# Feed-forward: seven quarter products for the first matrix from the second pair of column groups on, in place of the third

## The chip, the cores and the metric

The kernel runs on one core of a Trainium2 chip. The metric is the device time of one execution in microseconds (us). A run is timed several times and the median is quoted. "TensorE" is the matmul engine (PE in the rows, PEld its weight loads), "VectorE" is DVE, "ScalarE" is ACT, "GpSimd" is POOL, and "SyncE" is SP, whose queue here issues the weight loads from device memory.

## The reference

Two blocks of two layers each are computed one after the other over 512 tokens of width 1024. Only one piece matters here, the feed-forward that closes each of the two layers of the second block:

```python
def swiglu(x, w1, w3, w2):
    return (jax.nn.silu(x @ w1) * (x @ w3)) @ w2

h = h + swiglu(rmsnorm(h, ffn_norm[layer]), ffn_w1[layer], ffn_w3[layer], ffn_w2[layer])
```

`w1` and `w3` are 1024 x 2816, `w2` is 2816 x 1024, everything is float32.

## The kernel before

Activations are kept transposed, features on the 128 partitions and tokens in the free dimension. Every dense product of float32 values is made of three float16 products: each operand is split into a high part (float16) and a low part (the rest, float16), and high x high, high x low, low x high are added in PSUM (`PASSES`). ScalarE writes the high part with a copy, VectorE the low part with a subtraction.

The weights come in groups of 256 columns (two blocks of 128, "column block 0 and 1") of 1024 rows, 1 MB, through a ring of two slots (`m.ring`), filled by SyncE; their high and low parts lie in `m.wsplit`, also two slots. The feed-forward (`ffn_window`) takes the groups in the order w1, w3, w1, w3, ... : a **pair** is one group of w1 (the silu matrix) and one of w3 (the gate matrix), so a pair yields 256 of the 2816 hidden features. There are eleven pairs (`KF // 2`, counted from 0 here).

- The **dense** pairs. For each column block, 8 steps of k times 3 passes of a 128x128 weight with all tokens. Pair 0 does this for the tokens in two halves, EARLY (0 to 255) and LATE (256 to 511), because the norm of the halves ends at different times; pair 1 has all 512 tokens at once. The result of w1 leaves PSUM through a silu on ScalarE (L2880), the result of w3 through a multiplication with it on VectorE (L2883). ScalarE and VectorE then split the hidden values (L2947, L2953).
- The **quick** pairs, class `Seven`. The product of a w1 group (1024 x 256, seen as 2 x 2 quarters B) with the normed input (2 x 2 quarters A: features by token halves) is made with seven quarter products P1 to P7 instead of eight, in the manner of Strassen. Each is 4 steps of k times 3 passes over 256 columns (L2637). They need sums of quarters of both sides: S1, S3, S2, S4 of the input, made once (`combine` L2761 on VectorE, high part L2774 on ScalarE, low part L2781 on VectorE), and T3, T1, T2, T4 of each w1 group (`sum_of` L2699 on VectorE), which are split with the two unsummed parts B11 and B2 in the order `SPLITS` (L2717 on ScalarE, L2724 on VectorE). VectorE adds the products up (L2800, L2805, L2811, L2816), ScalarE copies P1 (L2789) and applies the silus (L2823, L2826). The w3 group of a quick pair is dense over 512 tokens (L2649; split L2736 and L2746, gate L2835, hidden values L2842 and L2850).

The order on TensorE is P1, P2, P6, P7, P5, P3, P4, then gate block 0 and 1. What each needs:

```python
FACTORS = {"P1": ("B11", "A11", "B11"), "P2": ("B21", "A12", "B2"), "P3": ("B22", "S4", "B2"), "P4": ("T4", "A22", "T4"),
           "P5": ("T1", "S1", "T1"), "P6": ("T2", "S2", "T2"), "P7": ("T3", "S3", "T3")}
SPLITS = ("B11", "B2", "T3", "T1", "T2", "T4")
MIXED = ("S1", "S3", "S2", "S4")
```

PSUM has eight banks. The dense parts go round banks 0 to 5: first twelve parts of the residual product before the feed-forward (L2534 stores them), then pair 0's eight (EARLY silu 0, 1, EARLY gate 0, 1, LATE silu 0, 1, LATE gate 0, 1), then in the kernel before pair 1's four. `Seven` puts P1 and P5 in bank 0, P2 and P6 in bank 1, P7 in bank 2, P3 and P4 in bank 3, the gates in banks 4 and 5. In its first pair P1, P2, P7, P3 and the gates wait until the last dense part that used their bank is stored (`before`, which is `earlier` in `ffn_window`). The stores count on two semaphores, one for ScalarE (`da`) and one for VectorE (`dd`).

The order on each engine is written by hand as a table of times: every step `yield`s the time at which it is due, and `weave` merges the steps of an engine's streams by these times when the program is built. The times are a plan only: on the chip each engine runs its instructions in the woven order, with waits on semaphores. The times the change touches are those of `sum_time`, `split_time`, `combine`, `combine_hi` and `combine_lo`. `LED` in `ffn_window` is the number of dense pairs.

## Time and profile before

| | |
|---|---|
| median of 3 runs | 3083.76 us (3080.12 to 3085.23) |
| the profiled execution: its time | 3088.69 us |
| its span in the profile | 3086.9 us |
| TensorE busy | 2950.7 us, 96% |
| VectorE busy | 1836.0 us, 59% |
| ScalarE busy | 1310.4 us, 42% |
| mean granted TensorE clock | 0.984 of 2.4 GHz |

The profile is of one execution; starts are counted from the beginning of its span. The time of a run is a little longer than its span (1.8 us here). The quarter products of the first feed-forward run from 2087 to 2263 us, those of the second from 2784 to 2960 us. The duration of a matmul in a row includes its passage through the array, which overlaps the next one; the pace is read from the distance of starts.

### The profile page before, as it was taken

To read this page: it belongs to the slowest core of one execution; us is meant where nothing else is said; L and a number is where in the kernel's file an instruction comes from. 1 tells how busy PE (TensorE), PEld (TensorE's weight loads), DVE (VectorE), ACT (ScalarE), POOL (GpSimd) and SP (SyncE) were. 2 spreads that over 40 slices of the span, in tenths; PEclk is the share of its full clock that TensorE was granted. 3 is DMA by queue.
4 is the path that set the end of the run, shared out by engine and by line. 5 is a ranking of instruction groups with operands and counts; after the bars stand their busy time and mean duration, and the time that the engine had idled before them with its cause. 6 is when DMAs were issued, how large, how long until landed. Compare 5 with 4: busy or idle time off the path is not lost. (4 is left out here: it accounts for less than half of the span.)

```text
span 3086.9 us, 48857 instructions
## 1 busy us (share of the span) xinstructions
PE 2950.7 (96%) x19588; PEld 1860.2 (60%) x19588; DVE 1836.0 (59%) x3400; ACT 1310.4 (42%) x2743; POOL 35.7 (1%) x108
## 2 busy tenths in 40 slices
PE   7999999999999999999999988999999989999998
PEld 4576867766656466757554454366655666666654
DVE  6337665555534637765665567677734468777744
ACT  3235545443332325455444353444423238744422
POOL 0000000000000000000000000000000001100000
PEclk9999999999999999999999999999999989999999
DMA  8411112211122221122322323223324420023322
GB/s 335 178 59 43 42 62 73 94 68 52 49 105 85 101 86 57 42 90 69 130 82 106 110 95 113 92 83 110 110 94 128 139 74 2 17 94 110 110 94 84
DMA packets 59364, 282.98 MB, mean 92 GB/s; under 512 B 7773, under 2 KB 13533, under 8 KB 38533
## 3 DMA queue, kind: packets, MB, share of 16 engines
q1 hardware_dynamic: 54485, 274.49, 25.6%
q10 hardware_dynamic: 4656, 5.38, 0.5%
q8 instruction: 157, 2.57, 0.3%
q14 instruction: 66, 0.54, 0.1%
HBM read 261.83 MB, written 6.34 MB: 87 GB/s over the span
## 5 line engine op out<-in xcount | busy, mean ns | idle before, releaser
L315 PE MATMUL banks<-h_sb,wsplit_sb 128*128 128x512 f16 (+2 forms) x6528 | 1216.7, 340 | 44.7 <-PEq L86 18.3
L315 PEld LDWEIGHTS banks<-h_sb,wsplit_sb 128*128 128x128 f16 x6528 | 634.0, 99 | 537.5 <-issue 68.5
L315 PE MATMUL banks<-quads,wsplit_sb 128*128 128x512 f16 (+2 forms) x3300 | 587.4, 337 | 4.6 <-PEq L86 4.6
L300 DVE SCALAR_TENSOR_TENSOR wsplit_sb<-ring_sb,wsplit_sb 128x1024 f16<-128x1024 f32 (+2 forms) x356 | 382.5, 1090 | 251.6 <-ACT wsplit_sb L290 249.5
L290 ACT ACTIVATE wsplit_sb<-ring_sb 128x1024 f16<-128x1024 f32 (+2 forms) x356 | 330.1, 944 | 469.0 <-PE banks L315 419.4
L315 PEld LDWEIGHTS banks<-quads,wsplit_sb 128*128 128x128 f16 x3300 | 321.2, 98 | 254.1 <-issue 8.4
L315 PE MATMUL banks<-wsplit_sb,h_sb 128*128 128x256 f16 x2112 | 240.1, 273 | 0.0
L315 PEld LDWEIGHTS banks<-wsplit_sb,h_sb 128*128 128x128 f16 x2112 | 206.2, 98 | 29.5 <-issue 3.8
L2649 PE MATMUL banks<-h_sb,wsplit_sb 128*128 128x512 f16 x864 | 189.4, 379 | 0.0
L539 ACT ACTIVATE quads<-banks 128x256 f32<-128x256 f32 (+2 forms) x174 | 79.8, 461 | 192.3 <-PE banks L315 192.1
L2649 PEld LDWEIGHTS banks<-h_sb,wsplit_sb 128*128 128x128 f16 x864 | 84.4, 98 | 98.2
L1889 ACT ACTIVATE work_sb<-banks 128x512 f32<-128x512 f32 (+1 forms) x80 | 44.2, 553 | 120.6 <-PE banks L1903 88.0
L2534 DVE SCALAR_TENSOR_TENSOR x_sb<-banks,x_sb 128x512 f32<-128x512 f32 (+1 forms) x42 | 23.6, 563 | 101.3 <-PE banks L315 101.3
L386 ACT ACTIVATE work_sb<-x_sb 128x256 f32<-128x256 f32 (+1 forms) x80 | 33.8, 429 | 88.9 <-DVE x_sb L2534 45.2
L1177 DVE TENSOR_REDUCE small_sb<-banks 128x2 f32<-128x1536 f32 (+1 forms) x40 | 61.7, 1542 | 16.4 <-PE banks L623 15.9
L1182 ACT ACTIVATE work_sb<-banks,small_sb 128x768 f32<-128x768 f32 (+1 forms) x80 | 64.3, 811 | 16.0 <-DVE small_sb L1178 15.8
L3266 ACT ACTIVATE work_sb<-work_sb,small_sb 128x128 f32<-128x128 f32 (+3 forms) x128 | 70.2, 552 | 1.7 <-DVE small_sb L3257 1.7
L584 DVE SCALAR_TENSOR_TENSOR work_sb<-work_sb,banks 128x512 f32<-128x512 f32 (+1 forms) x24 | 14.3, 597 | 82.9 <-PE banks L315 82.9
L623 PE MATMUL banks<-quads 64*128 64x256 f32 (+1 forms) x288 | 56.6, 505 | 6.2 <-ACT work_sb L1182 4.6
L3257 DVE CUSTOM_DVE_ANT_0 work_sb<-banks,GB_sb 128x128 f32<-128x128 f32 (+3 forms) x128 | 57.3, 486 | 7.6 <-PE banks L3245 7.2
L3302 ACT ACTIVATE h_sb<-banks 128x128 f32<-128x128 f32 (+3 forms) x128 | 51.3, 427 | 22.1 <-PE banks L3291 22.1
L3291 PE MATMUL banks<-ident_sb,quads 128*128 128x128 f32 x320 | 51.7, 292 | 9.1 <-ACT h_sb L3302 8.0
(398 smaller groups left out, 3637.4 us busy)
## 6 DMA issues: line engine op xcount, KB each, us to landing
ring_sb<-in_w_in SPq DMA_DIRECT2D x52, 1024.0 KB, 4.9
ring_sb<-in_w_ffn SPq DMA_DIRECT2D x44, 1024.0 KB, 4.8
ring_sb<-in_w_merge SPq DMA_DIRECT2D x48, 768.0 KB, 4.4
ring_sb<-in_w_ffn SPq DMA_DIRECT2D x32, 704.0 KB, 4.0
quads<-in_w_mod SPq DMA_DIRECT2D x12, 1024.0 KB, 23.4
x_sb<-in_w_mod SPq DMA_DIRECT2D x12, 1024.0 KB, 7.1
ring_sb<-in_w_ab SPq DMA_DIRECT2D x12, 1024.0 KB, 4.8
ring_sb<-in_w_nsa SPq DMA_DIRECT2D x10, 1024.0 KB, 5.8
```

The lines of the kernel that those rows point to most:

```text
L290: act.activation(m.wsplit[:, s, 0, half * n:half * n + n], m.ring[:, s, half * n:half * n + n], ACT.Copy, scale=WSCALE).then_inc(w.hi[s], 1)
L300: dve.scalar_tensor_tensor(m.wsplit[:, s, 1, half * n:half * n + n], m.ring[:, s, half * n:half * n + n], WSCALE, m.wsplit[:, s, 0, half * ...
L315: mm = pe.matmul(p.bank, *p.terms(k, pw, px), start=(p.opens and k == 0 and z == 0), stop=(p.closes and k == p.depth - 1 and z == 2))
L539: return {"act": lambda eng, p: eng.activation(out, p, func, scale=UNSCALE), "dve": lambda eng, p: eng.tensor_scalar(out, p, UNSCALE, None ...
L623: mm = pe.matmul(self.region(u)[:, a:b], lhsT, rhs, start=True, stop=True, skip_group_check=True)
L1177: step(dve.tensor_reduce(mx, reg[:, 0:2 * unit.off].rearrange("p (c k) -> p c k", c=2)[:, :, 0:unit.nk], AX.X, ALU.max))
L1182: act.activation(E[:, u % 2, c * unit.nk:(c + 1) * unit.nk], reg[:, c * unit.off:c * unit.off + unit.nk], ACT.Exp, bias=sm[:, u % 2, 2 + c ...
L2649: mm = pe.matmul(self.m.ps[:, 4 + j, 0:S], self.m.wsplit[:, self.s1, pw, k * GC + j * P:k * GC + (j + 1) * P], part(self.m.h, px, k, 0, S) ...
L3257: dve.tensor_tensor_reduce(E[u % R][:, c, 0:nk], ps[:, 2 * (u % 2) + c, 0:nk], mask[:, S - nk:S], -SCALE64, 3.0e38, ALU.add, ALU.min, x[:, ...
L3266: act.activation(E[u % R][:, c, 0:nk], E[u % R][:, c, 0:nk], ACT.Exp, bias=x[:, 2 + c:3 + c], scale=-1.0, accum_out=x[:, 4 + c:5 + c]).the ...
L3291: out = pe.transpose(ps[:, 4 + c, b * P:(b + 1) * P], W[u % R][:, c, b * P:(b + 1) * P], m.ident[:, :])
L3302: act.activation(WT[u % R][:, c * nk:(c + 1) * nk], ps[:, 4 + c, 0:nk], ACT.Copy).then_inc(copied, 1)
```

## The change

`LED` becomes 1: pair 1 is handled by `Seven` (ten quick pairs, not nine), in both feed-forwards. The due times of the first quick pair's sums and splits and of the combinations of the input are moved with it, closer together.

```diff
     def sum_time(self, i, n):
-        return (self.at(i - 1) + 3.0 if i else self.t0 - 9.5) + 0.9 * n
+        return (self.at(i - 1) + 3.0 if i else self.t0 - 6.5) + 0.9 * n
 
     def split_time(self, i, n):
-        return (self.at(i - 1) + SEVEN if i else self.t0 - 9.0) + (0.2, 0.9, 2.1, 2.9, 3.7, 4.5)[n]
+        return (self.at(i - 1) + SEVEN if i else self.t0 - 5.0) + (0.2, 0.9, 2.1, 2.9, 3.7, 4.5)[n]
...
-            yield norms[1].t0 + 14.0 + 3.0 * i
+            yield norms[1].t0 + 11.2 + 1.3 * i
...
-            yield norms[1].t0 + 15.4 + 3.0 * i
+            yield norms[1].t0 + 12.4 + 1.3 * i
...
-            yield norms[1].t0 + 16.6 + 3.0 * i
+            yield norms[1].t0 + 13.6 + 1.3 * i
...
-    LED = 2
+    LED = 1
```

How the order moves, first on TensorE, at the end of pair 0 of the first feed-forward. `ml_delta_7` is the semaphore that VectorE's dense stores raise, `ml_kw_7` that of ScalarE's, `lo0_3` and `lo1_3` those of the weights' low parts in slots 0 and 1, `mn_hi_8` that of the low parts of B11, T3, T1 and T2, `op_da_5` that of the low parts of the combinations. Before:

```order
L315 MATMUL banks<-h_sb,wsplit_sb 128x256 [waits ml_kw_7,lo1_3]
L315 MATMUL banks<-h_sb,wsplit_sb 128x256 x23
L315 MATMUL banks<-h_sb,wsplit_sb 128x512 [waits ml_delta_7,lo0_3]
L315 MATMUL banks<-h_sb,wsplit_sb 128x512 x23
L315 MATMUL banks<-h_sb,wsplit_sb 128x512 [waits ml_delta_7,lo0_3]
L315 MATMUL banks<-h_sb,wsplit_sb 128x512 x23
```

And now:

```order
L315 MATMUL banks<-h_sb,wsplit_sb 128x256 [waits ml_kw_7,lo1_3]
L315 MATMUL banks<-h_sb,wsplit_sb 128x256 x23
L2637 MATMUL banks<-h_sb,wsplit_sb 128x256 [waits ml_delta_7,mn_hi_8]
L2637 MATMUL banks<-h_sb,wsplit_sb 128x256 x11
L2637 MATMUL banks<-h_sb,wsplit_sb 128x256 [waits ml_delta_7,lo0_3]
L2637 MATMUL banks<-h_sb,wsplit_sb 128x256 x11
L2637 MATMUL banks<-quads 128x256 [waits op_da_5,mn_hi_8]
L2637 MATMUL banks<-quads 128x256 x11
```

P1 and P2 (the first two groups of twelve of L2637) follow LATE gate 1 directly, where pair 1's silu products stood.

The second place is VectorE behind the last residual part of the norm (L441) of the same feed-forward. `work_sb<-ring_sb` and `ring_sb<-ring_sb` at L2699 are differences of weight quarters, L2883 over 256 columns the stores of LATE gate 0 and 1:

```order
 L441 TENSOR_TENSOR h_sb<-quads,h_sb 128x256 x2
 L2761 TENSOR_TENSOR quads<-quads 128x4x256
-L300 SCALAR_TENSOR_TENSOR wsplit_sb<-ring_sb,wsplit_sb 128x1024 x2
+L2699 TENSOR_TENSOR work_sb<-ring_sb 128x512
+L2761 TENSOR_TENSOR quads<-quads 128x4x256
+L2699 TENSOR_TENSOR ring_sb<-ring_sb 128x4x128
+L2781 TENSOR_TENSOR quads<-quads 128x1024
+L2699 TENSOR_TENSOR work_sb<-ring_sb 128x512
+L2761 TENSOR_TENSOR quads<-quads 128x4x256
+L2724 SCALAR_TENSOR_TENSOR wsplit_sb<-ring_sb,wsplit_sb 128x4x128
+L2699 TENSOR_TENSOR work_sb<-ring_sb,work_sb 128x512
+L2781 TENSOR_TENSOR quads<-quads 128x1024
```

The third is what follows there. The new listing goes on:

```order
L2761 TENSOR_TENSOR quads<-quads 128x4x256
L2724 SCALAR_TENSOR_TENSOR wsplit_sb<-ring_sb,wsplit_sb 128x1024
L2883 SCALAR_TENSOR_TENSOR GB_sb<-banks,GB_sb 128x256
L2781 TENSOR_TENSOR quads<-quads 128x1024
L2724 SCALAR_TENSOR_TENSOR quads<-work_sb,quads 128x512
L2724 SCALAR_TENSOR_TENSOR wsplit_sb<-ring_sb,wsplit_sb 128x4x128
L2953 TENSOR_TENSOR quads<-GB_sb,quads 128x512
L2781 TENSOR_TENSOR quads<-quads 128x1024
L2724 SCALAR_TENSOR_TENSOR quads<-work_sb,quads 128x512
L2883 SCALAR_TENSOR_TENSOR GB_sb<-banks,GB_sb 128x256
L2724 SCALAR_TENSOR_TENSOR quads<-work_sb,quads 128x512
L2953 TENSOR_TENSOR quads<-GB_sb,quads 128x512
```

The first of the two stores of pair 0's LATE gates stood behind one combination and two weight halves of 1024, the second besides behind one low part of a combination, a second combination and one L2953. Now both stand behind all four combinations and all four quarter differences, and the second behind all low parts but T4's. GpSimd's and SyncE's listings are the same before and after.

## Rows read from the trace of the kernel before

**Rows 1.** The page, part 1: busy time, share of the span, instructions

```profile
PE 2950.7 (96%) x19588; PEld 1860.2 (60%) x19588; DVE 1836.0 (59%) x3400; ACT 1310.4 (42%) x2743; POOL 35.7 (1%) x108
```

**Rows 2.** Timeline of TensorE, both feed-forwards: start us, us, engine, line, operation, count

```profile
2059.32 28.30 PE L315 MATMUL banks<-h_sb,wsplit_sb 128*128 128x256 f16 x162 [0.23 <-DVE h_sb L441]
2087.45 2.78 PE L2637 MATMUL banks<-h_sb,wsplit_sb 128*128 128x256 f16 x24
...
2756.10 28.30 PE L315 MATMUL banks<-h_sb,wsplit_sb 128*128 128x256 f16 x162 [0.23 <-DVE h_sb L441]
2784.24 2.78 PE L2637 MATMUL banks<-h_sb,wsplit_sb 128*128 128x256 f16 x24
...
2793.41 10.52 PE L2649 MATMUL banks<-h_sb,wsplit_sb 128*128 128x512 f16 x48
2803.76 2.78 PE L2637 MATMUL banks<-h_sb,wsplit_sb 128*128 128x256 f16 x24
```

**Rows 3.** Timeline of VectorE, first feed-forward, from the end of the norm

```profile
2059.70 0.99 DVE L441 TENSOR_TENSOR h_sb<-quads,h_sb 128x256 f16<-128x256 f32 x2
2060.79 1.23 DVE L2761 TENSOR_TENSOR quads<-quads 128x1024 f32<-128x1024 f32 x1
...
2065.47 0.42 DVE L2883 SCALAR_TENSOR_TENSOR GB_sb<-banks,GB_sb 128x256 f32<-128x256 f32 x1
2065.81 1.22 DVE L2781 TENSOR_TENSOR quads<-quads 128x1024 f16<-128x1024 f32 x1
2066.94 1.22 DVE L2761 TENSOR_TENSOR quads<-quads 128x1024 f32<-128x1024 f32 x1
2068.08 0.68 DVE L2953 TENSOR_TENSOR quads<-GB_sb,quads 128x512 f16<-128x512 f32 x1
2068.68 0.42 DVE L2883 SCALAR_TENSOR_TENSOR GB_sb<-banks,GB_sb 128x256 f32<-128x256 f32 x1
...
2082.01 0.68 DVE L2699 TENSOR_TENSOR work_sb<-ring_sb 128x512 f32<-128x512 f32 x1
2082.61 1.22 DVE L2724 SCALAR_TENSOR_TENSOR wsplit_sb<-ring_sb,wsplit_sb 128x1024 f16<-128x1024 f32 x1
2083.75 0.68 DVE L2699 TENSOR_TENSOR work_sb<-ring_sb,work_sb 128x512 f32<-128x512 f32 x1
```

**Rows 4.** Timeline of ScalarE in the same stretch

```profile
2061.75 1.06 ACT L290 ACTIVATE wsplit_sb<-ring_sb 128x1024 f16<-128x1024 f32 x1 [1.52 <-PE banks L315]
...
2068.20 1.06 ACT L2774 ACTIVATE quads<-quads 128x1024 f16<-128x1024 f32 x1 [1.64 <-DVE quads L2761]
2069.16 1.04 ACT L290 ACTIVATE wsplit_sb<-ring_sb 128x1024 f16<-128x1024 f32 x1
```

**Rows 5.** Weight loads of the first feed-forward: SyncE's timeline; issues, KB, us to landing

```profile
2040.97 62.37 SPq L196 DMA_DIRECT2D ring_sb<-in_w_ffn  x7
...
ring_sb<-in_w_ffn SPq DMA_DIRECT2D x7, 1024.0 KB, 4.8
```

**Rows 6.** TensorE after idle times: its timeline; windows (us, busy times, PEclk, DMA, GB/s)

```profile
1046.78 9.34 PE L315 MATMUL banks<-h_sb,wsplit_sb 128*128 128x512 f16 x30 [3.36 <-PEq L86]
...
1795.87 3.54 PE L315 MATMUL banks<-h_sb,wsplit_sb 128*128 128x256 f16 x18 [4.03 <-PEq L86]
...
1805.96 6.21 PE L315 MATMUL banks<-h_sb,wsplit_sb 128*128 128x256 f16 x40 [2.16 <-DVE wsplit_sb L300]
...
1045.00:1046.00 1.00, 0.00 (x0) 0.00 (x0) 0.83 (x2) 0.13 (x1) 0.00 (x0) 0.73 0.00 0
1046.00:1047.00 1.00, 0.22 (x1) 0.14 (x2) 0.68 (x2) 0.00 (x0) 0.00 (x0) 0.50 0.00 0
...
1052.00:1053.00 1.00, 1.00 (x6) 0.36 (x5) 0.96 (x2) 1.00 (x3) 0.00 (x0) 0.86 1.06 412
...
1796.00:1797.00 1.00, 1.00 (x8) 0.82 (x7) 0.91 (x3) 0.76 (x3) 0.00 (x0) 0.69 0.41 78
...
1799.00:1800.00 1.00, 1.00 (x5) 0.88 (x4) 0.96 (x4) 1.00 (x3) 0.00 (x0) 0.60 1.09 369
```

## The prediction, made before the changed kernel had run

> **What bounds the kernel now.** I read the page's busy shares first. TensorE works 2950.7 of 3086.9 us, VectorE 1836.0 [rows 1], so over the whole program TensorE is the bound and VectorE has slack. That average says nothing about the stretch that the change touches, so I went to the timeline of TensorE in the first feed-forward. There the dense part of the first two pairs runs without a break from 2059.32 to the first quarter product at 2087.45, and the second feed-forward repeats it, from 2756.10 to 2784.24 [rows 2]: every offset between the two is 696.8 us, so I work the first and count it twice. In steady state a pair takes 2803.76 - 2784.24 = 19.52 us, of which the seven quarter products (84 matmuls over 256 columns) take 9.17 us, 1.31 us each, and the 48 full matmuls of the gate matrix 10.35 us, 0.2156 us each [rows 2].
>
> Next comes VectorE's timeline in the same stretch [rows 3]. The reader is to see that the last residual part of the norm ends at about 2060.7, that the first combination of the normed input (L2761) starts at 2060.79, and that VectorE's instructions start in program order, one as soon as the one before permits. The store of a finished gate product (L2883, 256 columns) at 2065.47 sits in that queue like any other. The start-to-start distances are what I use as prices: 1.14 us for a combination or for the low part of a combination (L2761, L2781), 0.60 us for a difference of weight quarters (L2699) or anything else over 512 elements, 1.14 us for the 1024-element low part of weights (L2724), 0.34 us to start after the 256-column store, which itself lasts 0.42 us [rows 3].
>
> **What the change takes away.** The first matrix of pair 1 was 48 full matmuls, 10.35 us; it becomes 84 quarter ones, 9.17 us. Saved: 1.18 us in each feed-forward, 2.36 us together. That is the whole gain, 0.08%, less than the 0.2% (6.2 us) that a measurement of this kernel can tell from no change. So the sign hangs on what the earlier start costs.
>
> One rule of the skill speaks against even this gain. The rows give 0.109 us for 256 columns and 0.2156 us for 512 [rows 2]. The Trainium skill (TensorE: Matmul & The Clock Gate, Back-to-back issue gap) gives for a stream with weight loads some 131 ns at 512 columns and 81 ns at 128, so by an estimate on the line between them, 98 ns at 256, the quarter form would take 8.2 us against 6.3 and lose 1.9 us. The trace does not agree, and the measured rows stand; the 9.17 us hold the weight loads of 84 products already, so as a rival this has no chance left.
>
> **When TensorE wants pair 1.** Pair 1's dense part is 96 matmuls of 0.2156 us before 2087.45, so pair 0 ends on TensorE at 2066.75. Before the change nothing had to be ready there but ordinary weight halves. Now P1 is next. Its bank is 0. Counting the parts (12 residual, 8 of pair 0, six banks in turn) bank 0 was last used by the late gate product of column block 0 and bank 1 by that of block 1. Both are emptied by VectorE's L2883. P1 waits for the first such store, P2 for the second: the listing of TensorE shows both quarter products with a wait on the dense stores' semaphore of VectorE. In the old order pair 1 used banks 2 to 5, so banks 0 and 1 were free long before.
>
> **When VectorE gets to these two stores.** I lay the new listing over the prices, from 2060.79, which nothing in the change moves. Ahead of the first store stand four combinations (4 x 1.14 = 4.56), four quarter differences (4 x 0.60 = 2.40), two low parts of combinations (2.28), B11's low part (0.60) and B2's (1.14): 10.98 us. It starts at 2071.77 and ends at 2072.19. Behind it and ahead of the second come two low parts of combinations (2.28), those of T3, T1 and T2 (1.80), one low half of the hidden values L2953 (0.60), and the first store's own 0.34: 5.02 us. The second store starts at 2076.79 and ends at 2077.21. In all it is 16.0 us of work that VectorE must do before P2 may run, while TensorE comes for P1 after 6 us.
>
> ScalarE must not be late for this. It can begin the weights of pair 1 at 2061.75, when the late silu product is done [rows 4]. Its high parts cost 0.96 us for 1024 elements [rows 4], less than VectorE's 1.14 us for the low one. Step by step in the new listing each high part is done before VectorE comes for it: B11 by 2064.2 against 2067.15, B2 by 2066.1 against 2070.63, S2 by 2068.3 against 2072.1, the hidden values' by 2072.9 against 2074.45. So VectorE is never held and costs exactly its own work. The weights themselves are long there: SP's order is the same, and they land 4.8 us after the issue at 2041 [rows 5].
>
> **The path.** TensorE starts P1 at 2072.25 (0.06 us after the store's end), 5.5 us late. P1 is over at 2073.56 and P2 starts at 2077.27, another 3.7 us. P6 wants S2 and T2: T2's low part ends at 2076.87, so it finds all it needs; P7, P5, P3, P4 too (the copy of P1, L2789, has some 2 us to spare before P5 at 2081.2). From 2077.27 six products of 1.31 us and the gate's 10.35 us give 2095.48 for pair 1's end, where it was 2087.45: **8.03 us later in each feed-forward**, 9.2 us of waiting less the 1.18 saved.
>
> What is late next? Pair 2's weights are loaded when T4's low part is done, some 2077.8, and land 4.8 us later [rows 5], at 2082.7; VectorE has pair 2's parts ready by about 2093, TensorE asks for P1 at 2095.5. Covered, by about 7 us for B11 and 5 for B2; from there on a pair costs 19.52 us as before. ScalarE's additions (a copy and two silus of pairs of blocks for two silus) lie under the products. Both cost nothing.
>
> **The clock.** After idle stretches the granted clock falls from 2.4 to 1.2 GHz. After 4.03 us idle, up to 1795.87, it is low for (0.62 + 1 + 1 + 0.8) = 3.4 us (two windows at 0.50 lie between the rows shown), all in work: 1.7 us lost. After 3.36 us idle, up to 1046.78, it is low from 1045.5 to 1052.3, 5.5 us of it in work: 2.8 us lost. After only 2.16 us idle, up to 1805.96, it fell as well [rows 6]. Here come 5.5 us idle, a product of 1.3 us (2.6 at low clock, which the second wait hides, since P2 hangs on VectorE) and 2.4 to 3.7 us idle. So I expect the low clock at P2, and price it between 1.7 and 2.8 us: 2.2. The bounds are 0 (the rise happens to come with P2) and 3.4 (a low stretch of 6.8 us lies wholly in work).
>
> **The sum.** 2 x (8.03 + 2.2) = 20.5 us. Against the profiled execution, 3088.69 us, that is 3109.2; that execution lies 4.9 us above the median of the runs, 3083.76, and the forecast is of the median: **3104.3 us**, 0.66% slower.
>
> **Rivals.**
> - *The banks are not the limit.* If stores of pair 0 came in time, P1 would still wait for B11 (low part over at 2067.8), P2 for B2 (2071.85) and P6 for T2 (2076.87), since all hang on the same VectorE queue. Then pair 1 ends at 2076.93 + 5 x 1.31 + 10.35 = 2093.83, 6.4 us late, and with 2.2 for the clock the time is 3083.76 + 17.2 = 3101. For it: the same queue. Against: the order of the listing. In the new profile P6 would be what waits last, not P2. Chance 0.08.
> - *VectorE keeps up* (the other side). The gain of 2.36 us stays if the second store ends by 2068.1, when P1 is over, and T2's low part by 2069.4: 3081.4 us, inside 0.2%. For it: in steady state VectorE idles 1 to 2 us several times in a pair, and before the change it did not hold TensorE here at all. Against: it would have to do 16.0 us of listed work in about 7. The price turns positive for this change from the point where the second store is over 1.2 us late, and I find 9. It needs prices far below the measured ones or an order other than the listing. Chance 0.05.
> - *The clock stays low* through all seven products, because the stretch with two waits leaves TensorE little busy for longer than any in the trace: 7.9 us lost in each feed-forward in place of 2.2, 3083.76 + 2 x 15.9 = 3115.6. Against: at most 6.8 us low after the waits of rows 6, partly idle. Chance 0.07.
> - *The change does not do what it says*: the listing shows the 96 full matmuls of pair 1 gone from L315, and 84 quarter ones (L2637) and 48 full ones (L2649) in their place, in each feed-forward, so this has no chance left.
>
> **How the numbers follow.** Forecast 0.80, banks 0.08, VectorE 0.05, clock 0.07. Prediction 3104.3 us. Low end: clock at 0 gives 3099.8, the banks' rival with 0 clock 3096.5; high end: clock 3.4 twice gives 3106.6, and 2 to 3 us for the spread of the runs shown (3080.12 to 3085.23) carry it to 3109. The range of 3096 to 3109 holds the first two cases, 0.88 together less what a mis-sized price takes. Slower by over 0.2% (above 3089.9) 0.94, within 0.2% 0.05, faster 0.01.
>
> **What would show it.** TensorE's timeline near 2066.7 and near 2763.5 should show the L2637 products in two pieces: a wait of about 5.5 us ended by VectorE's L2883, twelve matmuls, a wait of 2.4 to 3.7 us ended by L2883 again, then no wait until the gates. VectorE should be busy without a gap from 2060.8 to 2078. The granted clock should be 0.5 for 3 to 7 us in each. Wrong would be: no L2883 among those for whom L2637 waits (then banks, or all, fall), a first L2637 before 2070, or a distance between pair 1 and 2 other than 19.5 us behind that stretch.

## The result and the profile after

The changed kernel takes 3108.53 us, the median of four runs (3105.88 to 3116.48), against 3084.3 us for the kernel before, the median of four runs beside it: the ratio is 1.0082 with a 95% interval of 1.0061 to 1.0103, or 19 to 32 us more. The profiled execution took 3110.99 us, its span is 3109.2 us. Below are the page of the changed kernel, part 1, and from part 5 the group of the quarter products whose inputs are the normed input and plain weights (P1 and P2 among them):

```profile
PE 2954.4 (95%) x19660; PEld 1866.9 (60%) x19660; DVE 1849.6 (59%) x3424; ACT 1313.8 (42%) x2753; POOL 35.8 (1%) x108
...
L2637 PE MATMUL banks<-h_sb,wsplit_sb 128*128 128x256 f16 x480 | 59.7, 283 | 15.4 <-DVE GB_sb L2883 15.4
```

TensorE has 72 matmuls more and 3.7 us more of busy time than in [rows 1], although less work was given to it. The last column says what became of the rest: 15.4 us of idle time just before these products, ended by VectorE's L2883. The waits of TensorE from 2060 to 2110 us (engine, line, waited for: us in total, times, longest) show half of it, the first feed-forward's:

```profile
PE banks L2637 <- DVE GB_sb L2883: 7.7, 2, 5.4
```

The timeline of TensorE in the first feed-forward answers to [rows 2]:

```profile
2064.43 7.58 PE L315 MATMUL banks<-h_sb,wsplit_sb 128*128 128x256 f16 x66 [0.23 <-DVE h_sb L441]
2077.44 2.72 PE L2637 MATMUL banks<-h_sb,wsplit_sb 128*128 128x256 f16 x12 [5.42 <-DVE GB_sb L2883]
2082.45 1.47 PE L2637 MATMUL banks<-h_sb,wsplit_sb 128*128 128x256 f16 x12 [2.29 <-DVE GB_sb L2883]
2083.75 2.78 PE L2637 MATMUL banks<-quads 128*128 128x256 f16 x24
...
2090.30 10.52 PE L2649 MATMUL banks<-h_sb,wsplit_sb 128*128 128x512 f16 x48
2100.66 2.78 PE L2637 MATMUL banks<-h_sb,wsplit_sb 128*128 128x256 f16 x24
```

Where 96 full matmuls followed pair 0 without a gap, TensorE now stands still for 5.42 us, does P1's twelve matmuls, and stands still for another 2.29 us. From P2 on nothing is missing until pair 2 begins at 2100.66. The second feed-forward repeats the waits to the hundredth:

```profile
2781.22 2.72 PE L2637 MATMUL banks<-h_sb,wsplit_sb 128*128 128x256 f16 x12 [5.43 <-DVE GB_sb L2883]
2786.23 2.72 PE L2637 MATMUL banks<-h_sb,wsplit_sb 128*128 128x256 f16 x12 [2.29 <-DVE GB_sb L2883]
2788.74 3.65 PE L2637 MATMUL banks<-quads 128*128 128x256 f16 x24
...
2796.15 10.52 PE L2649 MATMUL banks<-h_sb,wsplit_sb 128*128 128x512 f16 x48
```

It differs behind them: P2 to the gates takes 9.92 us here and 7.85 us in the first. That is the clock, and the windows show it (us, busy times of TensorE, weight load, VectorE, ScalarE, GpSimd, then the granted clock):

```profile
2078.00:2079.00 1.00, 1.00 (x7) 0.70 (x5) 1.00 (x3) 1.00 (x3) 0.00 (x0) 0.50 0.00 0
...
2082.00:2083.00 1.00, 0.55 (x6) 0.52 (x7) 0.90 (x3) 0.67 (x2) 0.00 (x0) 1.00 0.00 0
...
2786.00:2787.00 1.00, 0.77 (x4) 0.58 (x5) 0.90 (x3) 0.88 (x2) 0.00 (x0) 0.50 0.00 0
...
2790.00:2791.00 1.00, 1.00 (x9) 0.80 (x7) 0.00 (x0) 0.00 (x0) 0.00 (x0) 0.75 1.32 377
```

In the first feed-forward the clock is at 1.2 GHz for P1 and back before P2, so that only time which P2 waits out anyway is slow. In the second it is low into the slice from 2790, under P2 and much of P6 and P7.

VectorE's timeline answers to [rows 3]. From 2065.91 to the second store at 2081.87 its whole timeline has no gap; the lines show the start of the list and the two stores (L2883) in the middle and near the end of it:

```profile
2065.91 1.23 DVE L2761 TENSOR_TENSOR quads<-quads 128x1024 f32<-128x1024 f32 x1
...
2076.87 0.42 DVE L2883 SCALAR_TENSOR_TENSOR GB_sb<-banks,GB_sb 128x256 f32<-128x256 f32 x1
...
2081.87 0.43 DVE L2883 SCALAR_TENSOR_TENSOR GB_sb<-banks,GB_sb 128x256 f32<-128x256 f32 x1
...
2087.61 0.69 DVE L2699 TENSOR_TENSOR work_sb<-ring_sb 128x512 f32<-128x512 f32 x1 [1.65 <-DMA ring_sb<-in_w_ffn]
```

To compare kernels I use one measure from here on: the **stretch** from the start of the first combination (L2761) to the start of the second matrix's first product (L315, behind the last pair). It is 202.43 us in both feed-forwards of the kernel before. In the changed kernel it is 210.52 and 212.59: 8.09 and 10.16 us more, 18.2 together. The span has 22.3 us more; the other 4 lie in the rest of the program, whose instructions the change does not touch.

### The profile page after: what moved, and what is told of

Its sections match the earlier page's. It is cut to its first block and busy times, and to the rows that moved or that the text cites. A ratio compares the mean times of both kernels' runs of the same rounds, so it can differ in the third digit from the quotient of the medians.

```text
span 3109.2 us, 49055 instructions
## 1 busy us (share of the span) xinstructions
PE 2954.4 (95%) x19660; PEld 1866.9 (60%) x19660; DVE 1849.6 (59%) x3424; ACT 1313.8 (42%) x2753; POOL 35.8 (1%) x108
## 5 line engine op out<-in xcount | busy, mean ns | idle before, releaser
L315 PE MATMUL banks<-h_sb,wsplit_sb 128*128 128x512 f16 (+2 forms) x6336 | 1176.6, 339 | 45.3 <-PEq L86 18.3
L315 PEld LDWEIGHTS banks<-h_sb,wsplit_sb 128*128 128x128 f16 x6336 | 615.6, 99 | 517.8 <-issue 71.0
L315 PE MATMUL banks<-quads,wsplit_sb 128*128 128x512 f16 (+2 forms) x3300 | 588.8, 337 | 4.6 <-PEq L86 4.6
L290 ACT ACTIVATE wsplit_sb<-ring_sb 128x1024 f16<-128x1024 f32 (+2 forms) x348 | 321.7, 942 | 468.1 <-PE banks L315 408.9
L300 DVE SCALAR_TENSOR_TENSOR wsplit_sb<-ring_sb,wsplit_sb 128x1024 f16<-128x1024 f32 (+2 forms) x348 | 372.7, 1087 | 246.5 <-ACT wsplit_sb L290 244.3
L315 PEld LDWEIGHTS banks<-quads,wsplit_sb 128*128 128x128 f16 x3300 | 321.6, 98 | 255.0 <-issue 10.3
L315 PE MATMUL banks<-wsplit_sb,h_sb 128*128 128x256 f16 x2112 | 240.7, 273 | 0.0
L315 PEld LDWEIGHTS banks<-wsplit_sb,h_sb 128*128 128x128 f16 x2112 | 206.5, 98 | 30.3 <-issue 4.4
L2649 PE MATMUL banks<-h_sb,wsplit_sb 128*128 128x512 f16 x960 | 210.5, 379 | 0.0
L2649 PEld LDWEIGHTS banks<-h_sb,wsplit_sb 128*128 128x128 f16 x960 | 93.9, 98 | 109.0
L2637 PE MATMUL banks<-h_sb,wsplit_sb 128*128 128x256 f16 x480 | 59.7, 283 | 15.4 <-DVE GB_sb L2883 15.4
L2736 ACT ACTIVATE wsplit_sb<-ring_sb 128x1024 f16<-128x1024 f32 x40 | 41.9, 1048 | 55.5 <-PE banks L2649 55.5
L2637 PEld LDWEIGHTS banks<-h_sb,wsplit_sb 128*128 128x128 f16 x480 | 48.2, 101 | 27.6 <-issue 16.8
L2724 DVE SCALAR_TENSOR_TENSOR wsplit_sb<-ring_sb,wsplit_sb 128x512 f16<-128x512 f32 (+1 forms) x60 | 52.0, 867 | 17.8 <-ACT wsplit_sb L2717 17.7
```

The lines of the kernel that those rows point to most:

```text
L290: act.activation(m.wsplit[:, s, 0, half * n:half * n + n], m.ring[:, s, half * n:half * n + n], ACT.Copy, scale=WSCALE).then_inc(w.hi[s], 1)
L300: dve.scalar_tensor_tensor(m.wsplit[:, s, 1, half * n:half * n + n], m.ring[:, s, half * n:half * n + n], WSCALE, m.wsplit[:, s, 0, half * ...
L315: mm = pe.matmul(p.bank, *p.terms(k, pw, px), start=(p.opens and k == 0 and z == 0), stop=(p.closes and k == p.depth - 1 and z == 2))
L2637: mm = pe.matmul(self.bank(name), self.weight(w, pw, k), self.tokens(a, px, k), start=(k == 0 and z == 0), stop=(k == 3 and z == 2))
L2649: mm = pe.matmul(self.m.ps[:, 4 + j, 0:S], self.m.wsplit[:, self.s1, pw, k * GC + j * P:k * GC + (j + 1) * P], part(self.m.h, px, k, 0, S) ...
L2724: dve.scalar_tensor_tensor(self.place(name, 1), self.source(name), WSCALE, self.place(name, 0), ALU.mult, ALU.subtract).then_inc(self.made ...
```

## The experiments

Each was timed in five rounds beside the kernel before. In the table, "late" is the excess of the stretch, first and second feed-forward; P1, P2 and P6 are starts after the first combination in the first feed-forward; the ratio is to the kernel before, with its 95% interval. "Rest" is the span outside the two stretches.

| kernel | P1 | P2 | P6 | late, us | rest, us | median, us | ratio |
|---|---|---|---|---|---|---|---|
| before (first profile) | | | | 0, 0 | 2682.0 | 3083.76 | 1 |
| after (first profile) | 11.53 | 16.54 | 17.84 | 8.09, 10.16 | 2686.1 | 3108.53 | 1.0082 [1.0061, 1.0103] |
| again | 11.54 | 16.54 | 19.06 | 10.85, 9.91 | 2681.9 | 3110.61 | 1.0075 [1.0063, 1.0087] |
| control | | | | 0, 0 | 2686.2 | 3086.88 | 1.0004 [0.9994, 1.0013] |
| banks | 7.10 | 11.11 | 16.12 | 9.09, 8.04 | 2684.0 | 3106.30 | 1.0059 [1.0046, 1.0072] |
| stores | 8.41 | 12.42 | 17.10 | 9.02, 9.02 | 2680.9 | 3108.32 | 1.0065 [1.0053, 1.0077] |
| first_store | 8.07 | 17.18 | 19.70 | 10.92, 10.53 | 2679.2 | 3112.72 | 1.0083 [1.0068, 1.0099] |
| defer | 10.39 | 14.26 | 16.78 | 7.91, 7.50 | 2682.2 | 3101.80 | 1.0054 [1.0039, 1.0070] |
| dummies | 11.53 | 16.54 | 17.84 | 8.09, 8.09 | 2684.1 | 3107.69 | 1.0064 [1.0051, 1.0077] |
| second_only | | | | 6.33, 9.93 | 2678.5 | 3101.45 | 1.0047 [1.0033, 1.0061] |
| second_clean | | | | 0, 9.76 | 2676.5 | 3099.00 | 1.0037 [1.0025, 1.0049] |
| full | 5.94 | 7.94 | 9.26 | 3.33, 6.00 | 2699.7 | 3111.02 | 1.0077 [1.0061, 1.0092] |
| full2 | 5.94 | 7.94 | 9.26 | 4.18, 3.32 | 2684.2 | 3098.90 | 1.0037 [1.0023, 1.0050] |

### The changed kernel and the kernel before once more

The first question was the 4 us outside the feed-forwards. "again" is the changed kernel, "control" the kernel before, both unaltered, under new names.

> The changed kernel once more, unaltered, for its spread and a second profile. The first profile has the two feed-forwards 8.1 and 10.1 us longer (from the first combination L2761 to the first product of the second weight matrix), 18.2 together, and 4.9 us already lost ahead of the first combination, where nothing was changed. Theory A (that loss is the chance of the clock gate in stretches that both kernels have): here the feed-forwards are again 8 to 10.5 us longer each, the first combination starts anywhere from 2058 to 2067 us, and the time is 18 to 24 us above the kernel before. Theory B (the change does something to the part ahead of it): the first combination starts at 2065 us or later again.

> The kernel before, unaltered, for a second profile. Theory A: its first combination starts somewhere else than at 2060.8 us, by up to 5 us, with other low stretches of the clock; ratio 1.000 within 0.2%. Theory B: at 2060.8 within 1 us, since the early loss belongs to the changed kernel.

Measured: VectorE's timeline has the first combination of the changed kernel here:

```profile
2059.80 1.23 DVE L2761 TENSOR_TENSOR quads<-quads 128x1024 f32<-128x1024 f32 x1
```

and that of the kernel before, which had it at 2060.79 in [rows 3], here:

```profile
2068.28 1.23 DVE L2761 TENSOR_TENSOR quads<-quads 128x1024 f32<-128x1024 f32 x1
```

So the point at which the feed-forward begins moves by several microseconds from one execution to the next in either kernel, 2058.3 to 2068.3 over all profiles but full's. With it goes the time at the low clock ahead of that point: by the clock's record in the traces 44 us in the two profiles that come there at 2058.3 (defer and first_store), 51 in again, 68 in the changed kernel's first and 65 in control. The rest is 2686.2 us in control and 2681.9 in again, the reverse of the first pair. So the 4 us between the first two profiles need no effect of the change, and theory B is out: the changed kernel comes here at 2059.8, not at 2065 or later. Theory A had put the kernel before within 5 us of 2060.8; it came 7.5 us later. The stretch repeats far better. The kernel before has 202.43 us both times, and in "again" P1 and P2 start at 11.54 and 16.54 as before; only the clock differs, which was low over P2, P6 and P7 this time (TensorE's timeline of again):

```profile
2071.34 2.72 PE L2637 MATMUL banks<-h_sb,wsplit_sb 128*128 128x256 f16 x12 [5.43 <-DVE GB_sb L2883]
2076.34 2.72 PE L2637 MATMUL banks<-h_sb,wsplit_sb 128*128 128x256 f16 x12 [2.29 <-DVE GB_sb L2883]
2078.86 4.33 PE L2637 MATMUL banks<-quads 128*128 128x256 f16 x24
```

### Banks: is the PSUM bank the limit?

The quarter products take other banks, as pair 1 of the kernel before did, so that P1 and P2 need none that VectorE still has to empty.

```diff
-        b, half = {"P1": (0, 0), "P5": (0, 0), "P2": (1, 0), "P6": (1, 1), "P7": (2, 0), "P4": (3, 0), "P3": (3, 1)}[name]
+        b, half = {"P1": (2, 0), "P5": (2, 0), "P2": (3, 0), "P6": (3, 1), "P7": (0, 0), "P4": (1, 0), "P3": (1, 1)}[name]
...
-                    pe.wait_ge(*(self.before(0) if i == 0 else (self.added, 4 * i - 2)))
+                    pe.wait_ge(*(self.before(2) if i == 0 else (self.added, 4 * i - 2)))
...
```

The other three `before` and the two `halves_of` (L2800, L2816) follow the banks.

> The quarter products change PSUM banks so that P1 and P2 of the first quick pair use banks 2 and 3, whose last stores are old, and P7 and P3 wait for the two late gate stores. Theory Q (VectorE's queue as a whole is the limit, 16 us of work): P1 waits for B11's low part, P2 for B2's, P6 for T2's; each feed-forward is 6.4 us longer than before plus 0 to 2 us of clock, so 13 to 17 us in all, 1.5 to 5 us less than the changed kernel. Theory W (only the two bank waits cost): the stall is gone, each feed-forward 1.2 us shorter than before, the time 2 us below the kernel before.

TensorE's timeline of banks:

```profile
2067.70 1.48 PE L2637 MATMUL banks<-h_sb,wsplit_sb 128*128 128x256 f16 x12 [0.99 <-DVE wsplit_sb L2724]
2071.71 2.43 PE L2637 MATMUL banks<-h_sb,wsplit_sb 128*128 128x256 f16 x12 [2.53 <-DVE wsplit_sb L2724]
2076.72 5.30 PE L2637 MATMUL banks<-quads 128*128 128x256 f16 x24 [2.57 <-DVE quads L2724]
```

The stores are gone as releasers, and in their place stand VectorE's low parts: B11 for P1, B2 for P2, T2 for P6. P2 comes 5.4 us earlier than in the changed kernel, but P6 only 1.7 us. This is the rival of the prediction on the banks, to its number: it had P6 at 16.14, measured 16.12. The bank was what TensorE waited for last, and behind it stood the same queue. The kernel is late by 9.09 and 8.04 us; 6.4 of each were forecast without the clock, so by that sum 1.6 to 2.7 us of each belong to the clock.

### Stores: the same question by the order alone

The banks stay, and VectorE does the two stores as soon as pair 0 has produced them.

```diff
-            yield p.t1
+            yield p.t1 + getattr(p, "shift", 0.0)
...
+        f1[6].shift, f1[7].shift = -3.24, -4.69
```

> The banks stay, but VectorE issues the two late gate stores early, the first behind the second combination, the second behind the first low part of a combination and T2's difference. Theory Q: P1 waits for B11's low part, P2 for B2's, P6 for T2's, all some 0.8 us later than with other banks, since the stores and a short wait for the product stand ahead of them: each feed-forward about 7.2 us longer than before plus 0 to 2 of clock, 14 to 19 us in all. Theory W: no wait, 2 us below the kernel before.

TensorE's timeline of stores:

```profile
2070.09 1.48 PE L2637 MATMUL banks<-h_sb,wsplit_sb 128*128 128x256 f16 x12 [2.31 <-DVE wsplit_sb L2724]
2074.09 1.48 PE L2637 MATMUL banks<-h_sb,wsplit_sb 128*128 128x256 f16 x12 [2.53 <-DVE wsplit_sb L2724]
2078.77 4.45 PE L2637 MATMUL banks<-quads 128*128 128x256 f16 x24 [3.19 <-DVE quads L2724]
```

The same three releasers as in banks, and P6 0.7 us earlier than in the changed kernel. Two different edits that free the bank in time both end at T2. The limit is the sum of what VectorE has to do before the third product, not the bank.

### First store: one of the two waits

Only the first store is moved ahead (`f1[6].shift, f1[7].shift = -3.24, 0.0`).

> As the changed kernel, but only the first late gate store is early, so P1 is freed (it then waits for B11's low part, some 8 us after the first combination instead of 11.5) and P2 is not. If the second wait decides, P2 starts 16.5 to 17 us after the first combination as in the changed kernel (a little later by the 0.4 us that VectorE waits for the gate product), and the feed-forwards are as long as there, 210.5 to 213.5 us. If the two waits cost each their own, each feed-forward is 3 to 5 us shorter.

TensorE's timeline of first_store:

```profile
2066.36 1.48 PE L2637 MATMUL banks<-h_sb,wsplit_sb 128*128 128x256 f16 x12 [1.97 <-DVE wsplit_sb L2724]
2075.47 2.72 PE L2637 MATMUL banks<-h_sb,wsplit_sb 128*128 128x256 f16 x12 [7.63 <-DVE GB_sb L2883]
```

P1 comes 3.5 us earlier and P2 0.6 us later: what one wait loses the next one gains, 7.63 us in place of 2.29. Of two waits in series on one queue, the last decides.

### Defer: a dose

The fourth combination (S4, whose product P3 comes sixth) is moved behind the first stores. Nothing else changes, so VectorE has 2.28 us less to do before the second store.

```diff
-            yield norms[1].t0 + 11.2 + 1.3 * i
+            yield norms[1].t0 + 11.2 + 1.3 * i + (3.8 if i == 3 else 0.0)
...
-            yield norms[1].t0 + 12.4 + 1.3 * i
+            yield norms[1].t0 + 12.4 + 1.3 * i + (2.8 if i == 3 else 0.0)
...
-            yield norms[1].t0 + 13.6 + 1.3 * i
+            yield norms[1].t0 + 13.6 + 1.3 * i + (1.6 if i == 3 else 0.0)
```

> As the changed kernel, but the fourth combination and its parts (S4, wanted only by the fifth of six products after P2) stand behind the second late gate store: 2.28 us less VectorE work ahead of P2. Theory Q: P2 starts 2.28 us sooner after the first combination (14.3 us instead of 16.5), P1 1.14 us sooner, each feed-forward 2.28 us shorter than in the changed kernel, 4.6 us together. Against it: if something else than VectorE's amount of work set P2's start, nothing or less.

TensorE's timeline of defer:

```profile
2068.72 2.72 PE L2637 MATMUL banks<-h_sb,wsplit_sb 128*128 128x256 f16 x12 [4.29 <-DVE GB_sb L2883]
2072.59 2.72 PE L2637 MATMUL banks<-h_sb,wsplit_sb 128*128 128x256 f16 x12 [1.15 <-DVE GB_sb L2883]
```

P2 starts at 14.26 in place of 16.54: 2.28 us taken from the queue, 2.28 us gained at P2, by two waits that become 1.13 and 1.14 us shorter. The stretches were to be 2.28 us shorter too, and this came out only in part: 7.91 and 7.50 us late against 8.09 and 10.16 in the changed kernel's first profile. With the clock at full speed the stretch would be late by 8.03 - 2.28 = 5.75 us; it was by 7.91 and 7.50, so the low clock took 2.2 and 1.8 us. The time follows: 1.0054 against 1.0075 in again, though the intervals overlap a little.

### Dummies: the clock by itself

Products that nobody reads, into a bank that is not in use then, fill the two waits: 50 before P1 and 24 before P2. The lines below are four further down than in the changed kernel, the dummies' own is L2624.

```diff
+                if i == 0 and name in ("P1", "P2"):
+                    for q in range(50 if name == "P1" else 24):
+                        pe.matmul(self.m.ps[:, 6, 0:HALF], part(self.m.h, 0, 0, 0, P), part(self.m.h, 0, 0, 0, HALF),
+                                  start=True, stop=True)
```

> As the changed kernel, with 50 products of 256 columns into an unused bank ahead of P1 and 24 ahead of P2, of operands that are there: TensorE is busy in the two waits. Clock theory: no low clock in either feed-forward, P1 to P4 at 1.31 us each, each feed-forward 8.0 us longer than before, the 2 us that the second one lost to the clock are back. If the loss had another cause than the clock, the second feed-forward stays about 10 us longer. The dummies take 5.45 and 2.6 us, so P1 starts within 0.2 us and P2 within 0.3 us of their times without them.

TensorE's timeline of dummies, and one of its windows:

```profile
2068.61 5.62 PE L2624 MATMUL banks<-h_sb 128*128 128x256 f16 x50
2074.20 1.47 PE L2641 MATMUL banks<-h_sb,wsplit_sb 128*128 128x256 f16 x12
2075.50 2.78 PE L2624 MATMUL banks<-h_sb 128*128 128x256 f16 x24
2079.20 1.47 PE L2641 MATMUL banks<-h_sb,wsplit_sb 128*128 128x256 f16 x12 [0.92 <-DVE GB_sb L2887]
```

```profile
2074.00:2086.00 12.00, 11.08 (x102) 9.57 (x100) 10.20 (x15) 4.55 (x8) 0.00 (x0) 1.00 0.42 149
```

P1 and P2 start exactly where they did (11.53 and 16.54): they hang on VectorE alone. The granted clock stays at 1.00 over the whole place, and the stretch is late by 8.09 us in **both** feed-forwards, where 8.03 had been forecast for the waits. What the changed kernel loses beyond 8.09 (0 and 2.07 in one profile, 2.76 and 1.82 in the other) is the clock. The ratio, 1.0064, lies below the two of the changed kernel, 1.0075 and 1.0082, by about as much as that (3.4 to 5.5 us for two stretches), but the intervals overlap.

### One feed-forward only

In second_only the first feed-forward has two dense pairs again, with the change's due times (`LED = 2 - l`); in second_clean it has the due times of the kernel before too, so that this feed-forward is wholly as before.

> The change in the second feed-forward alone, the first has two dense pairs as before. Theory: half the cost, the first feed-forward 0 us longer, the second 8.0 to 10.5, the time 8 to 12 us above the kernel before. The times at which combinations and sums are due are the new ones in both, which alone should cost the first nothing within 0.3 us.

> The change in the second feed-forward alone, now with the old due times in the first. Theory: first feed-forward 202.4 us as before, the second 210.5 to 213.3 as in the changed kernel, the time 8 to 11 us above the kernel before, half of the change's cost. In the earlier run of this kind the first feed-forward cost 6.3 us by the new due times alone.

TensorE's timeline of second_only, first feed-forward:

```profile
2068.25 23.80 PE L315 MATMUL banks<-h_sb,wsplit_sb 128*128 128x512 f16 x96 [3.25 <-DVE wsplit_sb L300]
```

The forecast of nothing for the first feed-forward was wrong. The due times alone, with no quick pair, already cost 6.33 us: the combinations now stand ahead of dense pair 1's own weight halves (L300), TensorE waits 3.25 us for these, and by the trace's clock record it runs at 1.2 GHz for 6.8 us from 2067.3 on, most of it behind the wait. This kernel is therefore no clean half of the change; second_clean is. TensorE's timeline of it, second feed-forward:

```profile
2763.59 2.72 PE L2637 MATMUL banks<-h_sb,wsplit_sb 128*128 128x256 f16 x12 [5.42 <-DVE GB_sb L2883]
```

Its first stretch is 202.43 us, to the hundredth that of the kernel before, the second is 9.76 us late, and the time is 1.0037: 7.7 to 15.1 us more for one feed-forward, about half of what the changed kernel loses. The loss lies in the feed-forward that has the change, and the two add up.

### Full and full2: can the pair be made to pay?

If VectorE's list is what bounds, a version that pays must have nearly all of it done before TensorE comes after 6 us. Both kernels take the banks of the experiment above, do both stores early, split T2 second and S2's low part first, and give the first quick pair due times of its own. In full the four differences of weight quarters go to GpSimd for that pair; in full2 they are back on VectorE but in its idle time within the norm, the copy of P1 is due earlier on ScalarE, and the hidden values' low parts (L2953) later.

```diff
-    SPLITS = ("B11", "B2", "T3", "T1", "T2", "T4")
+    SPLITS = ("B11", "T2", "B2", "T3", "T1", "T4")
+    LOWS = ("S2", "S3", "S1", "S4")
...
-                if (name in self.BY_POOL) == pool:
+                if (i == 0) == pool:
```

(full; in full2 the second hunk reads)

```diff
-                    yield self.sum_time(i, n)
+                    yield self.sum_time(i, n) if i else self.t0 + (-15.3, -14.15, -14.12, -3.7)[n]
```

> The cure, if VectorE's work in this place is the limit: the quarter sums of the first quick pair go to GpSimd (which idles) and are made while the norm runs, 2.4 us off VectorE; banks as in the run that moved them; the two late gate stores early; order on VectorE S1, S3, S2 made, B11, T2, S2, B2, T3, S3, then S4, T1, S1, S4, T4 in the order in which the products (P1, P2, P6, P7, P5, P3, P4) want them. By the prices, P1 starts at once, P2 0.3 us late, P5 0.6 us late, then no wait: each feed-forward 0.2 to 1.2 us shorter than before, the time 0 to 2.4 us below the kernel before, which is within what can be told from no change. Against it: GpSimd's sums slow VectorE's norm down, or a wait that I haven't found.

> The cure again, mended by what its first run showed: the four quarter sums of the first quick pair are back on VectorE, three of them in the idle times that the norm leaves it (0.55 us behind the reciprocal, 1.32 us behind the first two scalings), ScalarE's copy of P1 stands ahead of the rest of its splits, and the hidden values' low halves behind the gate weights. By the prices P1 starts at once (5.95 us after the first combination), P2 0.7 us late (7.9), P5 waits 0.6 us for S1, P3 0.5 us for S4, then nothing: the gates start 16.9 us after the first combination, each feed-forward takes 203.0 us from the first combination on, 0.6 more than before the change, with no low clock; the time is 1 us above the kernel before, which can't be told from no change. That is the bound of this place by VectorE's work: the saving of 1.18 us is spent on waits even in the best order I find.

Neither forecast came true. Full was to be 0.2 to 1.2 us shorter in each feed-forward, and its stretches are 3.33 and 6.00 us late; full2 was to be 0.6 us late, and is 4.18 and 3.32. In full P1 no longer waits (5.94), and P2 and P6 follow at 7.94 and 9.26, but its rest is 2699.7 us, some 14 more than the highest of the others. VectorE's timeline of full, while GpSimd is at the differences (lines one further down for all but the norm):

```profile
2053.99 1.49 DVE L428 SCALAR_TENSOR_TENSOR quads<-x_sb,vecs_sb,work_sb 128x256 f32<-128x256 f32 x1
2055.41 1.48 DVE L407 TENSOR_TENSOR work_sb<-work_sb 128x256 f32<-128x256 f32 x1
2056.81 1.48 DVE L441 TENSOR_TENSOR h_sb<-quads,h_sb 128x256 f16<-128x256 f32 x1
2058.21 2.28 DVE L300 SCALAR_TENSOR_TENSOR wsplit_sb<-ring_sb,wsplit_sb 128x1024 f16<-128x1024 f32 x1
```

and GpSimd's:

```profile
2053.05 2.15 POOL L2700 TENSOR_TENSOR work_sb<-ring_sb 128x512 f32<-128x512 f32 x1 [80.07 <-DMA ring_sb<-in_w_ffn]
2055.28 1.33 POOL L2700 TENSOR_TENSOR ring_sb<-ring_sb 128x512 f32<-128x512 f32 x1
2056.68 1.32 POOL L2700 TENSOR_TENSOR work_sb<-ring_sb 128x512 f32<-128x512 f32 x1
2058.09 1.32 POOL L2700 TENSOR_TENSOR work_sb<-ring_sb,work_sb 128x512 f32<-128x512 f32 x1
```

The same instructions take 0.48, 0.42, 0.42 and 1.22 us elsewhere in this kernel. Four of VectorE's instructions together lost 4.2 us. Three are the norm's, for which TensorE waits: 4.64 us, where it waits 1.50 us at the same place of the changed kernel, and the same again in the second feed-forward. That makes 6.3 us of the 14 or more. The rest was not taken apart; the low clock outside the stretches lasted 116 us in this profile and 65 to 100 us in all others. The norm's wait is the first of these lines of TensorE's timeline of full, and the second is another cost:

```profile
2058.35 1.46 PE L315 MATMUL banks<-h_sb,wsplit_sb 128*128 128x256 f16 x6 [4.64 <-DVE h_sb L441]
...
2088.05 2.78 PE L2638 MATMUL banks<-quads,wsplit_sb 128*128 128x256 f16 x24 [3.67 <-ACT GB_sb L2790]
```

With so much of VectorE's work gone, P5 waits for ScalarE's copy of P1, the next in the row. Full2 mends both in part (TensorE's timeline of full2):

```profile
2071.32 1.48 PE L2638 MATMUL banks<-h_sb,wsplit_sb 128*128 128x256 f16 x12 [0.52 <-DVE wsplit_sb L2725]
...
2075.97 1.47 PE L2638 MATMUL banks<-quads,wsplit_sb 128*128 128x256 f16 x12 [0.55 <-issue]
2077.71 1.47 PE L2638 MATMUL banks<-quads,wsplit_sb 128*128 128x256 f16 x12 [0.27 <-issue]
...
2081.39 10.53 PE L2650 MATMUL banks<-h_sb,wsplit_sb 128*128 128x512 f16 x48 [0.90 <-DVE wsplit_sb L2747]
...
2099.47 2.78 PE L2638 MATMUL banks<-quads,wsplit_sb 128*128 128x256 f16 x24 [2.26 <-ACT GB_sb L2790]
```

For P5 and P3 of pair 1 (2075.97, 2077.71) the rows name no releaser. VectorE's timeline of full2 has the low parts of S1 and S4 end 0.1 us ahead of them:

```profile
2074.66 1.22 DVE L2782 TENSOR_TENSOR quads<-quads 128x1024 f16<-128x1024 f32 x1
2076.39 1.22 DVE L2782 TENSOR_TENSOR quads<-quads 128x1024 f16<-128x1024 f32 x1
```

By distances of starts, each wait costs a little more than its bracket says: P2 0.69 us, P5 0.71, P3 0.43, the gates 1.06, and pair 2's P5 2.42, together 5.3 us; less the 1.18 saved this is 4.1, and the first stretch is 4.18 us late, with the clock at 2.4 GHz throughout. The forecast had the first three waits; the last two, 3.5 us, it had at nothing. Every wait is now small, each ends on another step, and the last is in the pair behind. Of the kernels tried that have the change in both feed-forwards this one loses least, and it is still 0.37% slower than the kernel before. To win, the five would have to shrink below 1.18 us together, for at most 2.36 us in all, under what a measurement tells from nothing.

## Why the prediction was right, and where it missed

The account of the feed-forwards was right. What failed is the step from them to the time of the whole kernel, told under **The sum**.

**What is taken away** (1.18 us in each): right. From P2 on six products take 7.85 us (2082.45 to 2090.30), the gates 10.36, and pair 2's seven quarter products 9.17 again (2100.66 to 2109.83). The added quarter products run at 0.109 us each. The rule of the Trainium skill weighed there (TensorE: Matmul & The Clock Gate, Back-to-back issue gap) stays contradicted by this.

**VectorE's queue**: right, and with the clock it is the whole mechanism within the stretches. Forecast from 2060.79 on, the stores were to let P1 start after 11.46 us and P2 after 16.48 us. Measured 11.53 and 16.54, in both feed-forwards and both profiles. The waits were 5.42 us (forecast 5.5) and 2.29 us (forecast 2.4 to 3.7, the lower value with P1 at half clock, which is what happened). Where the clock costs nothing, pair 1 ends 34.75 us after the first combination, forecast 34.69. Defer shows the cause of P2's late start by its dose, dummies shows the waits' cost without the clock: 8.09 us against the forecast 8.03.

**The banks' rival** was a true description of the next limit, not of this kernel: TensorE waited for the bank, and with the bank free it waits for T2 1.7 us earlier. **VectorE keeps up** and **the clock stays low through all seven products** did not occur. Nothing in pair 2 was late, as forecast; the load that VectorE waits for (1.65 us, at 2087.61) is in 13 us before TensorE begins pair 2.

**The clock** (2.2 us in each, bounds 0 and 3.4): the bounds on the loss held, the value is no constant. It was 0, 2.1, 2.8, 1.8 us in the four stretches of the two profiles of the changed kernel. The forecast of 4.4 us for both compares with 2.1 and 4.6. The length was too short: the clock was to be low for 3 to 7 us, 6.8 at most, and was for 3.4, 10.2, 13.7 and 10.2 us. The bound of 3.4 us held all the same, because much of that time fell into the waits. The two waits are the same in each; what differs is when the clock falls and when it comes back.

**The sum**: the two stretches were to be 20.5 us longer, and were 18.2 and 20.8 us, so its terms held. Against the profiled execution I had 3109.2 us, and it took 3110.99. The median came out at 3108.53 where I had 3104.3, and the ratio applied to 3083.76 gives 3109.0, at the very top of the range or just above it. The step that failed is the last one: it added the 20.5 us of the stretches to the median of three runs, put the rest of the program at no change, and left only "2 to 3 us for the spread of the runs shown (3080.12 to 3085.23)" above the clock's bound.

The runs showed two things in its place. First, three runs were too few to show the spread. The kernel before has single runs from 3080.1 to 3095.9 us (55 runs over all the comparisons, median 3085.6), the changed kernel from 3105.9 to 3116.5 us (nine runs, median 3110.6). By an estimate from this spread a median of three or four runs is uncertain by 2 us or so on either side, before and after, and the range allowed for it once. Second, the medians rise by more than the stretches. The ratios of the changed kernel make 25 and 23 us, the stretches of its two profiles 18.2 and 20.8; the 18.2 lie just below the interval of their ratio, which begins at 18.8. In the table it is the same: leaving out full, nine of the ten rows of altered kernels have a ratio that stands for more than the two "late" figures beside it. The excess is 2.5 us on average over the ten, though all the others but the 18.2 lie within their intervals. The profiles do not show where: the rest of the span is 2682.0 and 2686.2 us in the two of the kernel before, 2686.1 and 2681.9 us in the two of the changed kernel. Whether the change costs 2 us or more outside the feed-forwards, or the profiled executions were not typical ones, stays open.

## What to carry to other kernels

When a step is started earlier, lay the helper engine's listed work from the last fixed point to the store that frees what the step needs, and compare it with the time at which the bound engine arrives: 16.0 us of list against 6 us was read off before anything ran and held to 0.1 us. An engine that is busy 59% of the span can be 100% busy in the one stretch that matters. A wait that ends on a store is not mended by freeing that store or by giving another bank when the next operands stand in the same queue; take work out of the queue (in defer P2 came earlier by exactly what was taken out, though the clock kept a part of it from the time) and ask each time which step is next in the row. Last, bound the saving first: 1.18 us in each feed-forward does not pay for the 5.3 us of small waits that even the best order tried here left. And a time forecast from a median of three runs needs a range that covers the spread of both kernels: 15.8 us between single runs of the kernel before.

## What was not expected of the hardware

GpSimd held up VectorE. Beside GpSimd's subtractions of two SBUF operands (128 x 512, float32, 1.33 us; VectorE does the same in 0.68), VectorE's instructions took 1.48 to 1.49 us in place of 0.42 to 0.48, and one of 1.22 us took 2.28. The starts come 1.40 to 1.42 us apart on VectorE, and so do GpSimd's from the second on (2055.28, 2056.68, 2058.09), each engine one instruction in turn. Start plus duration tells more: VectorE's three instructions of 256 columns end 0.28 to 0.29 us after GpSimd's (2055.48 after 2055.20, 2056.89 after 2056.61, 2058.29 after 2058.00), and GpSimd's next ends 1.12 to 1.13 us after VectorE's, as if only one worked at a time and the rest of each duration were waiting. The Trainium skill (SBUF — State Buffer, SBUF: two separate sides) says that the two share a port pair, and that it is locked for a whole instruction and not divided, when a VectorE instruction reads both its operands from SBUF and the GpSimd instruction reads SBUF too. All eight instructions here are of these kinds, and the rows agree. No run here shows GpSimd's subtraction alone.

The start of the feed-forward lay between 2058.3 and 2068.3 us in kernels whose instructions up to there do the same work. A change of a few microseconds is therefore read within its stretch, where the kernel before repeats to the hundredth (202.43 us four times), and not from spans alone.

The low clock after the same two waits cost between nothing and 2.8 us. In the four stretches of the changed kernel P1 and P2 start at the same places; the 1.2 GHz lasted 3.4, 10.2, 13.7 and 10.2 us.
